# Branch gates by seven products from the fourth unit on, and the silu gate of three retention heads applied as they leave their banks

## The chip, the cores and the metric

The kernel runs on one core of a Trainium2 chip. The metric is device time in microseconds. The kernel before takes 2031.95 us (median of 3 runs, 2031.89 to 2031.98). TensorE is called PE here, VectorE DVE, ScalarE ACT, GpSimd POOL and SyncE SP, as in the profile. Line numbers (L2022) are those of the kernel before.

## The reference, cut to what matters

The reference is one encoder block (attention of two kinds between two feed-forward parts) followed by two hybrid layers and a last norm. 512 tokens, width 1024, float32 throughout. The change touches only the hybrid layers, and of these the end:

```python
a = diff_attention(...) * jax.nn.silu(az)
c = short_conv(cx, cb, cc, conv_w) * jax.nn.silu(cz)
r = retention(rq, rk, rv) * jax.nn.silu(rz)      # retention ends in rms_norm(out) over each head of 128

g = jax.nn.sigmoid(gates).reshape(b, s, 3, 1024) # gates = h @ w_in[:, 5632:], 3072 columns
merged = g[:, :, 0] * (a @ w_branch[0])
for i in range(1, 3):
    merged = merged + g[:, :, i] * (branches[i] @ w_branch[i])
return x + merged @ w_out
```

## The kernel before, in words

**Precision.** Every operand of a large product is kept as a high and a low part (names `_hi`, `_lo`), and a product is three matmuls: high by high, low by high, high by low (L2218 to L2220, and L2351 to L2353 in the seven-product form). A weight slab of 128 x 1024 is loaded by SP into `w_raw` (a ring of six slots), rounded by ACT to `w_hi` (L865), and POOL makes `w_lo = w_raw - w_hi` (L709). `w_lo` lies on the bytes of `w_raw`. SP loads a slab when PE has used the slab that held its slot before (`w_used`).

**The hybrid layer.** It is run twice. Projections and attention come first. Then 16 retention steps run between the convolution's projections: PE adds the outputs of four retention heads in banks 0 to 3, one head of 128 features by 512 tokens in each. Each finished head is squared (`out_squares`, ACT: `r_sq`, a copy of the head to `r_out`, then `sq_hi`), POOL makes `sq_lo`, PE averages the squares into the head's own bank (`mean_square`, L2728 and L2729), ACT takes the square root there (`out_root`), and DVE inverts it, multiplies `r_out` by it and by the silu gate `rz` (`normed_out`, L2022 to L2024). ACT has to load a table each time it changes between square root and sigmoid.

**The merge.** Twelve units follow in each layer. Unit nn handles branch nn mod 3 for a pair of 128-feature blocks: gate columns (two slabs), sigmoid (ACT, into `gate_sb`), branch product (one slab), then DVE multiplies and, for branches 1 and 2, adds (`merged`). A unit is done in one of two ways:

- classic, for nn < M0: two `feature_tile` calls of 8 x 3 matmuls with 512 columns each, 48 in all;
- by seven products, for nn from M0 on: the weight pair and the activations are cut into quarters, sums of quarters of the weights (`gate_w_sums` on DVE, `t_raw1` on POOL) and of the activations (`first_x_sums`, `last_x_sum`, `x_sum_low`, once per layer, DVE) are formed, and seven products of 4 x 3 matmuls with 256 columns replace the eight of the plain form: 84 matmuls. DVE then adds up the partial results before the sigmoids.

`M0` is 4 before. PE in such a unit waits for the low part of the first gate slab (`ready`), for the sums' low parts (`wsl_done`, `xsl_done`), and before the branch product for a low part that belongs to the next unit (`gate_sum_low`, L2140). POOL's `w_lo` for a seven-product unit comes after DVE's `gate_w_sums`, since the sums read `w_raw` (L836).

**Order.** Each engine's list is written out by hand, and engines meet at semaphores only. DVE's list in the first units is: `normed_out(0)`, `normed_out(1)`, then for each nn its extra work and `merged(nn)`; heads 2 and 3 are normed at nn = 1, `retained_low` (`br_lo`, L2016) comes at nn = 2, `first_x_sums` at nn = M0 - 2, and `last_x_sum`, three `x_sum_low`, `gate_w_sums(M0)` and `gate_sum_low(M0, 2)` at nn = M0 - 1. The lines that tie the extra work to M0 are:

```python
if nn == M0 - 2:
    first_x_sums(2 + l, 3 + l, ms_part, ms_raw)
if nn == M0 - 1:
    last_x_sum(2 + l, ms_part, ms_raw)
    ...
    gate_w_sums(M0)
```

Of the kernel before, what the change touches and what calls it, by code (L numbers as in the profile page):

```python
# [15 lines left out]
P = 128  # L16
# [14 lines left out]
M0 = 4  # L31
# [102 lines left out]
def build(nc, x, ffn1_pre_g, ffn1_post_g, ffn1_w_gate, ffn1_w_up, ffn1_w_down, mix_pre_g, mix_post_g,  # L134
# [4 lines left out]
    with ExitStack() as ctx:  # L139
# [215 lines left out]
        swap_in, swap_ready, count_in = sem("swap_in"), sem("swap_ready"), sem("count_in")  # L355
        decay_in = sem("decay_in")
# [45 lines left out]
        mean_ready, rqh_done, rql_done, rst_done, rrt_done = (sem("mean_ready"), sem("rqh_done"), sem("rql_done"),  # L402
# [446 lines left out]
        def _(act):  # L849
# [248 lines left out]
            act.activation(swap_r[:, :], swap_sb[:, :], ACT.Copy).then_inc(swap_ready, 1)  # L1098
# [79 lines left out]
            for l in range(LAYERS):  # L1178
# [98 lines left out]
                def out_squares(h):  # L1277

                    act.wait_ge(r_o_done, 16 * l + 8 * (h // 2) + 7 + h % 2)
                    if h > 0:  # L1280
                        act.wait_ge(rst_done, 4 * l + h)
                    link(act.activation(r_sq[:, :], bank[h][:, :], ACT.Square))
                    act.activation(r_out[:, h, :], bank[h][:, :], ACT.Copy)
                    act.activation(sq_hi[:, :], r_sq[:, :], ACT.Copy).then_inc(rqh_done, 1)
# [14 lines left out]
                for i in range(16):  # L1299
# [30 lines left out]
                    if i in (12, 13, 15):  # L1330
                        out_squares({12: 0, 13: 1, 15: 2}[i])
                out_root(0)
                out_root(1)
                gate(0, 0)
# [93 lines left out]
        def _(dve):  # L1428
# [463 lines left out]
            for l in range(LAYERS):  # L1892
# [196 lines left out]
                normed_out(0)  # L2089
                normed_out(1)  # L2090
# [117 lines left out]
        def _(pe):  # L2208
# [401 lines left out]
            for l in range(LAYERS):  # L2610
# [290 lines left out]
```

## Time and profile before

| what | value |
|---|---|
| median of 3 runs | 2031.95 us (2031.89 to 2031.98) |
| profiled execution, its own time | 2031.64 us |
| its span, first to last instruction | 2029.8 us |
| PE busy | 2013.9 us, 99% of the span |
| DVE busy | 1231.4 us, 61% |
| ACT busy | 953.3 us, 47% |
| POOL busy | 1016.4 us, 50% |
| granted PE clock | 1.000 of full speed |

The profiled execution spends 1.84 us outside its span. A busy share says how much of the span an engine had an instruction in flight. It is an average over stages that differ. A row of a timeline gives the start, the duration (ends of neighbours overlap, so the difference of two starts is the time that an instruction takes in a chain) and, in brackets, idle time before it and what ended it.

### The profile page before, as it was taken

To read this page: it belongs to the slowest core of one execution; us is meant where nothing else is said; L and a number is where in the kernel's file an instruction comes from. 1 tells how busy PE (TensorE), PEld (TensorE's weight loads), DVE (VectorE), ACT (ScalarE), POOL (GpSimd) and SP (SyncE) were. 2 spreads that over 40 slices of the span, in tenths; PEclk is the share of its full clock that TensorE was granted. 3 is DMA by queue.
4 is the path that set the end of the run, shared out by engine and by line. 5 is a ranking of instruction groups with operands and counts; after the bars stand their busy time and mean duration, and the time that the engine had idled before them with its cause. 6 is when DMAs were issued, how large, how long until landed. Compare 5 with 4: busy or idle time off the path is not lost.

```text
span 2029.8 us, 30533 instructions
## 1 busy us (share of the span) xinstructions
PE 2013.9 (99%) x11856; PEld 1752.5 (86%) x11856; DVE 1231.4 (61%) x2036; ACT 953.3 (47%) x1781; POOL 1016.4 (50%) x576
## 2 busy tenths in 40 slices
PE   9999999999999999999999999999999999999998
PEld 8999988877789999988888888899888888888997
DVE  7777730877848777812357573965333676568553
ACT  5454623467755554523444544443443445354442
POOL 4666644346753666744434443465534443264542
PEclk9999999999999999999999999999999999999999
DMA  6333322311133333323322222333332222223332
GB/s 190 107 107 106 104 95 93 123 42 32 32 104 113 107 105 105 104 94 102 121 84 73 73 83 73 94 104 98 111 130 84 83 74 73 83 84 94 105 114 73
DMA packets 244287, 191.65 MB, mean 94 GB/s; under 512 B 6448, under 2 KB 208816, under 8 KB 243760
## 3 DMA queue, kind: packets, MB, share of 16 engines
q1 hardware_dynamic: 244144, 189.70, 30.8%
q8 instruction: 95, 1.56, 0.3%
q14 instruction: 48, 0.39, 0.1%
HBM read 187.58 MB, written 2.10 MB: 93 GB/s over the span
## 4 chain that ended last, share of the span: by engine, by line
PE 94%; DVE 3%; ACT 1%; issue 1%; SPq 0%; DMA 0%; POOL 0%; DVEq 0%; ACTq 0%
PE bank L2218 20%; PE bank L2220 20%; PE bank L2219 20%; PE bank L2353 9%; PE bank L2352 9%; PE bank L2351 9%; PE bank L2212 3%; PE bank L2510 1%; PE bank L2678 1%; PE bank L2530 1%; PE bank L2537 1%; DVE xn L1446 0%; DVE x_tok L1451 0%; PE bank L2707 0%; PE bank L2709 0%
## 5 line engine op out<-in xcount | busy, mean ns | idle before, releaser
L709 POOL TENSOR_TENSOR w_lo<-w_raw,w_hi 128x1024 fp32r<-128x1024 f32 x216 | 533.3, 2480 | 473.8 <-ACT w_hi L865 471.8
L865 ACT ACTIVATE w_hi<-w_raw 128x1024 fp32r<-128x1024 f32 x271 | 283.1, 1053 | 197.1 <-DMA w_raw<-in_ffn_w_down 125.1
L2218 PE MATMUL bank<-xt_hi,w_hi 128*128 128x512 f32 (+1 forms) x640 | 243.3, 380 | 0.5
L2219 PE MATMUL bank<-xt_lo,w_hi 128*128 128x512 f32 (+1 forms) x640 | 239.3, 374 | 0.0
L2220 PE MATMUL bank<-xt_hi,w_lo 128*128 128x512 f32 (+1 forms) x640 | 239.3, 374 | 0.0
L2218 PE MATMUL bank<-w_hi,xt_hi 128*128 128x512 f32 (+1 forms) x456 | 178.2, 391 | 0.0
L2220 PE MATMUL bank<-w_hi,xt_lo 128*128 128x512 f32 (+1 forms) x456 | 174.5, 383 | 0.0
L2219 PE MATMUL bank<-w_lo,xt_hi 128*128 128x512 f32 (+1 forms) x456 | 174.3, 382 | 0.0
L2218 PEld LDWEIGHTS bank<-xt_hi,w_hi 128*128 128x128 f32 x640 | 120.5, 188 | 29.3 <-issue 6.7
L2220 PEld LDWEIGHTS bank<-xt_hi,w_lo 128*128 128x128 f32 x640 | 120.5, 188 | 22.0
L2219 PEld LDWEIGHTS bank<-xt_lo,w_hi 128*128 128x128 f32 x640 | 120.6, 188 | 19.6
L2218 PE MATMUL bank<-w_hi,h_hi 128*128 128x512 f32 x352 | 137.1, 390 | 0.0
L2219 PE MATMUL bank<-w_lo,h_hi 128*128 128x512 f32 x352 | 137.0, 389 | 0.0
L2220 PE MATMUL bank<-w_hi,h_lo 128*128 128x512 f32 x352 | 136.9, 389 | 0.0
L2351 PE MATMUL bank<-xs_hi,ws_hi 128*128 128x256 f32 x456 | 129.0, 283 | 0.0
L2352 PE MATMUL bank<-xs_lo,ws_hi 128*128 128x256 f32 x456 | 129.0, 283 | 0.0
L2353 PE MATMUL bank<-xs_hi,ws_lo 128*128 128x256 f32 x456 | 129.0, 283 | 0.0
L2353 PE MATMUL bank<-xt_hi,w_lo 128*128 128x256 f32 x432 | 122.3, 283 | 0.0
L2352 PE MATMUL bank<-xt_lo,w_hi 128*128 128x256 f32 x432 | 122.2, 283 | 0.0
L2351 PE MATMUL bank<-xt_hi,w_hi 128*128 128x256 f32 x432 | 122.2, 283 | 0.0
L1440 DVE RECIPROCAL stat<-stat 128x1 f32<-128x1 f32 x12 | 2.0, 163 | 185.7 <-ACT stat L889 185.7
L778 POOL TENSOR_TENSOR w_lo<-w_raw,w_hi 128x1024 fp32r<-128x1024 f32 x38 | 91.8, 2415 | 30.9 <-ACT w_hi L865 19.1
(398 smaller groups left out, 5579.4 us busy)
## 6 DMA issues: line engine op xcount, KB each, us to landing
w_raw<-in_w_in SPq DMA_DIRECT2D x132, 512.0 KB, 3.8
w_raw<-in_ffn_w_down SPq DMA_DIRECT2D x44, 512.0 KB, 3.4
w_raw<-in_ffn_w_gate SPq DMA_DIRECT2D x43, 512.0 KB, 3.8
w_raw<-in_ffn_w_up SPq DMA_DIRECT2D x43, 512.0 KB, 3.8
w_raw<-in_w_out SPq DMA_DIRECT2D x24, 512.0 KB, 3.4
w_raw<-in_w_branch SPq DMA_DIRECT2D x24, 512.0 KB, 3.5
w_raw<-in_w_qkv SPq DMA_DIRECT2D x16, 512.0 KB, 3.8
x_tok<-in_x SPq DMA_DIRECT2D x4, 512.0 KB, 6.9
```

What stands on the lines that cost most here:

```text
L709: pool.tensor_tensor(lo_slots[i], raw_slots[i], f32(hi_slots[i]), ALU.subtract).then_inc(lo_ready, 1)
L778: pool.tensor_tensor(lo_slots[i], raw_slots[i], f32(hi_slots[i]), ALU.subtract).then_inc(lo_ready, 1)
L865: act.activation(hi_slots[i], raw_slots[i], ACT.Copy).then_inc(hi_ready, 1)
L2212: ins = pe.matmul(dst[:, cols(k)], blk, ident[:, :], is_transpose=True)
L2218: pe.matmul(out_ap, ah, bh, start=first, stop=False)
L2219: pe.matmul(out_ap, ah, bl, start=False, stop=False)
L2220: return pe.matmul(out_ap, al, bh, start=False, stop=last)
L2351: pe.matmul(dst, wh, xh, start=k == 0 and not onto, stop=False, skip_group_check=onto)
L2352: pe.matmul(dst, wh, xl, start=False, stop=False, skip_group_check=onto)
L2353: ins = pe.matmul(dst, wl, xh, start=False, stop=k == 3, skip_group_check=onto)
L2510: ins = pe.matmul(score_bank(k, e)[:, :], a[rows, cols(c)], b[rows, :], start=part == 0, stop=part == 2)
L2530: ins = pe.matmul(bank[7][:, :].rearrange("p (e q) -> p e q", e=2), va_hilo[:, j, pair // 2, :], p[:, hf, :, j, :], start=j + part == 0, s ...
```

## The change

1. `M0` is 3 instead of 4: unit 3 of each layer is done by seven products. All that is tied to M0 comes one unit earlier: `first_x_sums` joins heads 2 and 3 at nn = 1, and the rest of the preparation joins `retained_low` at nn = 2.
2. For heads 0 to 2 ACT no longer copies the head to `r_out`. DVE writes `r_out = bank * rz` instead (`gated_out`, new semaphore `rg_done`), for heads 0 and 1 at retention steps 13 and 14, for head 2 between `normed_out(0)` and `normed_out(1)`. `mean_square` of these heads, which overwrites the bank, now also waits for `rg_done`. `normed_out` of these heads has one multiplication instead of two.
3. ACT's square roots of heads 0 and 1 stand ahead of `out_squares(2)`.
4. Two one-time semaphores, `swap_ready` and `mean_ready`, become one, `matrix_ready`.

```diff
-M0 = 4
+M0 = 3
...
                     link(act.activation(r_sq[:, :], bank[h][:, :], ACT.Square))
-                    act.activation(r_out[:, h, :], bank[h][:, :], ACT.Copy)
+                    if h == 3:
+                        act.activation(r_out[:, h, :], bank[h][:, :], ACT.Copy)
...
-                    if i in (12, 13, 15):
-                        out_squares({12: 0, 13: 1, 15: 2}[i])
+                    if i in (12, 13):
+                        out_squares(i - 12)
                 out_root(0)
                 out_root(1)
+                out_squares(2)
                 gate(0, 0)
...
                     link(dve.reciprocal(bank[h][:, :], bank[h][:, :]))
+                    if h < 3:
+                        dve.wait_ge(rg_done, 3 * l + h + 1)
+                        dve.tensor_tensor(r_out[:, h, :], bank[h][:, :], r_out[:, h, :], ALU.mult).then_inc(br_ready, 1)
+                        return
                     link(dve.tensor_tensor(r_out[:, h, :], bank[h][:, :], r_out[:, h, :], ALU.mult))
                     dve.tensor_tensor(r_out[:, h, :], r_out[:, h, :], rz[:, h, :], ALU.mult).then_inc(br_ready, 1)
-                    dve.wait_ge(br_ready, 8 * l + 4 + h + 1)
+
+                def gated_out(h):
+
+                    dve.wait_ge(z_done, 8 * l + 4 + h + 1)
+                    dve.wait_ge(rqh_done, 4 * l + h + 1)
+                    dve.tensor_tensor(r_out[:, h, :], bank[h][:, :], rz[:, h, :], ALU.mult).then_inc(rg_done, 1)
...
                         branch_low(i // 2 - 4)
+                    if i in (13, 14):
+                        gated_out(i - 13)
                     dve.wait_ge(r_s_done, 8 * l + i // 2 + 1)
...
                 normed_out(0)
+                gated_out(2)
                 normed_out(1)
...
                     pe.wait_ge(rql_done, 4 * l + h + 1)
+                    if h < 3:
+                        pe.wait_ge(rg_done, 3 * l + h + 1)
```

DVE at retention step 14, before (`ba_lo` is the low part of a turned block of branch a, `ret_a` the scores of this step):

```order
L2011 TENSOR_TENSOR ba_lo<-bank,ba_hi 128x4x128 [waits bth_done]
L2048 TENSOR_TENSOR ret_a<-bank,decay_sb 128x128 [waits r_h_done,r_l_done,r_s_done]
L2065 TENSOR_TENSOR y_sb<-bank,y_sb 128x512 [waits w_used]
L2068 TENSOR_TENSOR y_sb<-y_sb,cz_sb 128x512 [waits cz_done,yb_done]
L2074 TENSOR_TENSOR pt_lo<-ret_a,pt_hi 128x128 [waits r_h_done]
```

and DVE at the same place in the changed kernel (lines are its own):

```order
L2013 TENSOR_TENSOR ba_lo<-bank,ba_hi 128x4x128 [waits bth_done]
L2036 TENSOR_TENSOR r_out<-bank,rz 128x512 [waits rqh_done,z_done]
L2061 TENSOR_TENSOR ret_a<-bank,decay_sb 128x128 [waits r_h_done,r_l_done,r_s_done]
L2078 TENSOR_TENSOR y_sb<-bank,y_sb 128x512 [waits w_used]
L2081 TENSOR_TENSOR y_sb<-y_sb,cz_sb 128x512 [waits cz_done,yb_done]
L2087 TENSOR_TENSOR pt_lo<-ret_a,pt_hi 128x128 [waits r_h_done]
```

`gated_out(1)` stands between `ba_lo`, which PE waits for, and `ret_a`. PE's `mean_square(1)` waits for it too.

DVE from the norm of head 2 on, before: the rows end at the first operation of `merged(1)` (`ms_part` and `ms_raw` are the activation sums, `m_raw` the merged output):

```order
L2022 RECIPROCAL bank<-bank 128x512 [waits rrt_done]
L2023 TENSOR_TENSOR r_out<-bank,r_out 128x512 [waits dve_step]
L2024 TENSOR_TENSOR r_out<-r_out,rz 128x512 [waits dve_step]
L2022 RECIPROCAL bank<-bank 128x512 [waits rrt_done,br_ready]
L2023 TENSOR_TENSOR r_out<-bank,r_out 128x512 [waits dve_step]
L2024 TENSOR_TENSOR r_out<-r_out,rz 128x512 [waits dve_step]
L2107 TENSOR_TENSOR bank<-bank,gate_sb 128x512 [waits gs_done,w_used,br_ready]
```

and DVE there in the changed kernel:

```order
L2024 RECIPROCAL bank<-bank 128x512 [waits rrt_done]
L2027 TENSOR_TENSOR r_out<-bank,r_out 128x512 [waits rg_done,dve_step]
L2024 RECIPROCAL bank<-bank 128x512 [waits rrt_done]
L2029 TENSOR_TENSOR r_out<-bank,r_out 128x512 [waits dve_step]
L2030 TENSOR_TENSOR r_out<-r_out,rz 128x512 [waits dve_step]
L1549 TENSOR_TENSOR ms_part_86<-xt_hi,xt_lo 128x1024 [waits rst_done,xtl_done,r_o_done,ch_done]
L1549 TENSOR_TENSOR ms_part_88<-xt_hi,xt_lo 128x1024
L1564 TENSOR_TENSOR ms_raw_92<-ms_part_86,ms_part_88 128x1024 [waits dve_step]
L1549 TENSOR_TENSOR ms_part_85<-xt_hi,xt_lo 128x1024
L1567 TENSOR_TENSOR ms_raw_89<-ms_raw_92,ms_part_85 128x1024 [waits xs_made,dve_step]
L1568 TENSOR_TENSOR ms_raw_90<-ms_part_85,ms_part_86 128x1024
L2121 TENSOR_TENSOR bank<-bank,gate_sb 128x512 [waits gs_done,w_used]
```

The six operations of `first_x_sums` now stand between the last head and `merged(1)` (L2121 and L2124 there); before, they stood behind `merged(1)` and `retained_low`.

## Rows read from the trace of the kernel before

**Rows 1.** The page: PE's busy time, and the chain that ended last, by engine.
```profile
PE 2013.9 (99%) x11856; PEld 1752.5 (86%) x11856; DVE 1231.4 (61%) x2036; ACT 953.3 (47%) x1781; POOL 1016.4 (50%) x576
...
PE 94%; DVE 3%; ACT 1%; issue 1%; SPq 0%; DMA 0%; POOL 0%; DVEq 0%; ACTq 0%
```

**Rows 2.** Windows, units 1 to 5: length, PE, PEld, DVE, ACT, POOL, clock.
```profile
1275.94:1292.31 16.37, 16.37 (x74) 13.52 (x73) 15.06 (x10) 8.51 (x12) 9.90 (x5) 1.00 0.33 98
1292.31:1308.63 16.32, 16.32 (x74) 13.52 (x73) 15.93 (x14) 3.65 (x5) 9.20 (x4) 1.00 0.32 96
1308.63:1324.95 16.32, 16.32 (x74) 13.52 (x73) 12.70 (x14) 9.62 (x13) 5.51 (x4) 1.00 0.34 98
1324.95:1341.03 16.08, 15.78 (x109) 14.66 (x108) 10.77 (x17) 6.27 (x12) 11.41 (x7) 1.00 0.33 99
1341.03:1356.57 15.54, 15.54 (x109) 14.58 (x108) 9.04 (x16) 6.38 (x12) 9.52 (x7) 1.00 0.33 102
```

**Rows 3.** Waits of PE: total us, times, longest.
```profile
PE bank L2728 <- DVE ba_lo L2011: 0.8, 2, 0.4
PE bank L2218 <- DVE xt_lo L2140: 0.8, 2, 0.5
```

**Rows 4.** Timeline of PE: start, duration, operation, idle before and its releaser.
```profile
1257.39 0.50 PE L2728 MATMUL bank<-sq_hi,mean_r 128*128 128x512 f32 x1 [0.38 <-DVE ba_lo L2011]
```

**Rows 5.** Timeline of DVE, retention step 14.
```profile
1256.64 0.69 DVE L2011 TENSOR_TENSOR ba_lo<-bank,ba_hi 128x512 fp32r<-128x512 f32 x1 [8.03 <-ACT ba_hi L1270]
1257.25 0.28 DVE L2048 TENSOR_TENSOR ret_a<-bank,decay_sb 128x128 f32<-128x128 f32 x1
```

**Rows 6.** Timeline of ACT: squares of head 2, roots of heads 0, 1.
```profile
1263.89 0.60 ACT L1282 ACTIVATE r_sq<-bank 128x512 f32<-128x512 f32 x1 [2.58 <-PE bank L2220]
...
1266.96 1.07 ACT L1288 ACTIVATE bank<-bank 128x512 f32<-128x512 f32 x2
```

**Rows 7.** Timeline of DVE, from head 1 to unit 4.
```profile
1272.49 3.37 DVE L2022 RECIPROCAL bank<-bank 128x512 f32<-128x512 f32 x1
1275.89 0.69 DVE L2023 TENSOR_TENSOR r_out<-bank,r_out 128x512 f32<-128x512 f32 x1
1276.61 2.26 DVE L2024 TENSOR_TENSOR r_out<-r_out,rz 128x512 f32<-128x512 f32 x1
1278.91 1.29 DVE L2105 TENSOR_TENSOR m_raw<-bank,gate_sb 128x512 f32<-128x512 f32 x2
...
1292.56 0.70 DVE L2107 TENSOR_TENSOR bank<-bank,gate_sb 128x512 f32<-128x512 f32 x1 [1.32 <-PE bank L2220]
...
1295.24 4.69 DVE L2016 TENSOR_TENSOR br_lo<-r_out,br_hi 128x512 fp32r<-128x512 f32 x4
1299.85 4.55 DVE L1547 TENSOR_TENSOR ms_part<-xt_hi,xt_lo 128x1024 f32<-128x1024 f32 x2
1304.43 1.22 DVE L1562 TENSOR_TENSOR ms_raw<-ms_part,ms_part 128x1024 f32<-128x1024 f32 x1
...
1307.97 2.31 DVE L1566 TENSOR_TENSOR ms_raw<-ms_part,ms_part 128x1024 f32<-128x1024 f32 x1
...
1319.18 0.70 DVE L2133 TENSOR_TENSOR bank<-bank,w_raw 128x512 f32<-128x512 f32 x1
...
1326.95 0.68 DVE L2140 TENSOR_TENSOR t_lo<-bank,t_hi 128x512 fp32r<-128x512 f32 x1
```

**Rows 8.** Timeline of POOL, same stretch.
```profile
1273.56 12.28 POOL L709 TENSOR_TENSOR w_lo<-w_raw,w_hi 128x1024 fp32r<-128x1024 f32 x5
1292.94 5.23 POOL L709 TENSOR_TENSOR w_lo<-w_raw,w_hi 128x1024 fp32r<-128x1024 f32 x2 [7.09 <-ACT w_hi L865]
1299.57 2.61 POOL L709 TENSOR_TENSOR w_lo<-w_raw,w_hi 128x1024 fp32r<-128x1024 f32 x1 [1.40 <-ACT w_hi L865]
1307.27 1.94 POOL L831 TENSOR_TENSOR t_raw<-w_raw 128x512 f32<-128x512 f32 x1 [5.09 <-DMA w_raw<-in_w_in]
1320.02 3.25 POOL L836 TENSOR_TENSOR w_lo<-w_raw,w_hi 128x1024 fp32r<-128x1024 f32 x1 [10.81 <-DVE bank L2133]
```

More of the change, by code:

```diff
@@ L354, in build @@
         tabs1_in, tabs2_in = sem("tabs1_in"), sem("tabs2_in")
-        swap_in, swap_ready, count_in = sem("swap_in"), sem("swap_ready"), sem("count_in")
-        decay_in = sem("decay_in")
+        swap_in, matrix_ready, count_in = sem("swap_in"), sem("matrix_ready"), sem("count_in")
+        decay_in, rg_done = sem("decay_in"), sem("rg_done")
         ident_ready = sem("ident_ready")
@@ L401, in build @@
         fl_done = sem("fl_done")
-        mean_ready, rqh_done, rql_done, rst_done, rrt_done = (sem("mean_ready"), sem("rqh_done"), sem("rql_done"),
+        rqh_done, rql_done, rst_done, rrt_done = (sem("rqh_done"), sem("rql_done"),
                                                               sem("rst_done"), sem("rrt_done"))
@@ L1097, in _ @@
             act.wait_ge(swap_in, 48)
-            act.activation(swap_r[:, :], swap_sb[:, :], ACT.Copy).then_inc(swap_ready, 1)
+            act.activation(swap_r[:, :], swap_sb[:, :], ACT.Copy).then_inc(matrix_ready, 1)
             highs(S_UNIT)
@@ L2034, in _ @@
                 link(dve.memset(u_sb[:, 0:2], 0.0))
-                dve.memset(f32(mean_r[:, :]), 1.0 / P).then_inc(mean_ready, 1)
+                dve.memset(f32(mean_r[:, :]), 1.0 / P).then_inc(matrix_ready, 1)
                 dve.wait_ge(decay_in, 16 * (l + 1))
@@ L2557, in unit_swap @@
                 if j == 0:
-                    pe.wait_ge(swap_ready, 1)
+                    pe.wait_ge(matrix_ready, 1)
                 pe.wait_ge(uc_done, j + 1)
@@ L2725, in mean_square @@
                     if h == 0:
-                        pe.wait_ge(mean_ready, l + 1)
+                        pe.wait_ge(matrix_ready, l + 2)
                     pe.wait_ge(rql_done, 4 * l + h + 1)
+                    if h < 3:
+                        pe.wait_ge(rg_done, 3 * l + h + 1)
                     pe.matmul(bank[h][:, :], mean_r[:, :], sq_hi[:, :], start=True, stop=False)
```

## The prediction, made before the change was timed

> **What bounds the kernel now.** I read the page first: PE is busy 99% of the span, and 94% of the chain that ended last is PE's [rows 1]. So a change is worth what it takes from PE's own work, less what it adds to PE's waits. Then I cut layer 0's merge into windows of one unit, because that is where M0 acts [rows 2]. Units 1 to 3 are classic and last 16.32 us (unit 1: 16.37). Unit 5, by seven products, lasts 15.54. Unit 4, the first by seven products, lasts 16.08: 0.54 over unit 5. The same rows show DVE busy 15.06 and 15.93 of 16.3 us in units 1 and 2, and 12.70 in unit 3, the unit that goes. So DVE, idle over much of the kernel, is full just where the change takes a unit of cover away. The waits of PE [rows 3] give two places where DVE is late already, each twice (once a layer): `mean_square` behind `ba_lo`, and the branch product of the first seven-product unit behind L2140. After that I followed DVE and POOL row by row. All rows are of layer 0; layer 1 has the same waits at the same places, so the sum is made once and doubled.
>
> **PE's own work.** Unit 3 goes from 48 matmuls of 512 columns to 84 of 256. The windows have both kinds with the branch product in them: 16.32 - 15.54 = 0.78 us less a layer [rows 2]. The Trainium skill ("TensorE: Matmul & The Clock Gate", Back-to-back issue gap) gives the isolated spacing as N / 2.4 plus 2.5 ns: 109.2 ns for 256 columns, 215.8 for 512, so 48 x 215.8 - 84 x 109.2 = 1.19 us, an estimate by that page. By it the sum below would be 0.8 us lower over two layers. The windows measure the pair in this kernel, so 0.78 stands.
>
> **`gated_out(1)` before `mean_square(1)`.** PE starts L2728 at 1257.39, just behind `ba_lo`, which starts at 1256.64 and takes 0.69 [rows 4, 5]. Now `gated_out(1)` stands next on DVE. It starts where `ret_a` started, 0.61 after `ba_lo`, and I give it 0.69, as L2023, which also reads one bank and one SBUF tile [rows 7]. PE is released 0.61 us later. PE had no slack there, so this is a plain cost. Bounds: 0 if `ba_lo` were not the last releaser, 0.75 if it takes its whole duration. I take 0.61.
>
> **`gated_out(0)` and `gated_out(2)`: nothing.** Head 0's waits for `sq_hi`, which ACT now reaches sooner by one copy, and DVE is idle 8.03 us between steps 13 and 14 [rows 5]; that gap covers it. If it did not, the cost would be another 0.7. Head 2's follows `normed_out(0)`. ACT was idle for 2.58 us before the squares of head 2, that is from 1261.3 [rows 6]; three operations of some 0.6 and a table load, which fills the 1.3 us that are left up to 1266.96, preceded the roots. Now the load and the roots use the idle time: 1261.3 + 0.6 (`gated_out(1)` has moved DVE, and ACT behind it) + 1.3 = 1263.2, the first root 0.6 later. The reciprocal (3.40) and its multiplication (0.7) follow, so `gated_out(2)` ends near 1268.7, and PE's third mean square begins at about 1270 (unit 0's product of 24 matmuls and this stand before 1275.94). The squares of head 2 stay near 1264.4, since PE releases them, 0.6 later than before. The table loads are as many as before. That leaves 1.4 us of slack before it costs anything.
>
> **DVE's list up to the first seven-product unit.** Before, `merged(0)` began at 1278.91 because the two heads ahead of it were late [rows 7]; PE was through with that product about 1275.5. Now two multiplications and the 1.6 us that one of them lost (2.26 against 0.69 [rows 7]) are gone, so DVE waits for PE: 1275.5 + 0.61 + 0.25 (the lag seen at unit 1, 1292.56 against 1292.31 [rows 2, 7]) = 1276.3. From there, with differences of starts [rows 7]: `merged(0)` 1.2, to 1277.5. Heads 2 and 3: 3.40 + 0.72 and 3.40 + 0.72, to 1285.7, then head 3's last multiplication beside the end of POOL's five `w_lo` (1273.56 + 12.28 = 1285.84 [rows 8]), to 1286.5. Then comes, without a gap, everything from `first_x_sums` to `gate_w_sums`. Before, this ran from 1299.85 to 1319.18 + 0.70 = 1319.88: 20.03 us, one `merged` of four operations in it, as now. `retained_low` is added to it.
>
> Two sizes in it need a choice. The first two sums took 4.55 where their like takes 1.2 (the row at 1304.43), an excess of 2.1; `br_lo` took 4.69 for four, where 0.61 each makes 2.45, an excess of 2.2 [rows 5, 7]. Both lie beside POOL's `w_lo` [rows 8] (the instructions at 1292.94 and 1299.57). In the changed kernel POOL's run of `w_lo` has ended by 1285.84, and its next is held until `gate_w_sums` is done. The bounds are no excess and all of it, 4.3; I take none. L1566's excess of 1.1 beside `t_raw` stays, because `t_raw` falls into the same stretch. So 20.03 - 2.1 + 2.45 = 20.4, and `gate_w_sums` ends at 1306.9. The Trainium skill ("SBUF — State Buffer", Who interferes with whom) says that a DVE instruction with two SBUF inputs and a GpSimd one that reads SBUF exclude each other for a whole instruction. The trace agrees in that L2024 took 2.26 beside POOL's `w_lo`, while operations with a bank input there kept 0.69. By that rule the excess goes, by a reading as a lasting property of these operations it stays; the second is the rival below.
>
> **What PE then waits for in unit 3.** Without waits PE starts it at 1308.63 + 0.61 = 1309.24 [rows 2].
> - The low part of the first gate slab: POOL had it 3.39 us after `gate_w_sums` (1319.88 to 1320.02 + 3.25 [rows 7, 8]), and PE started unit 4 at 1324.95, 1.7 us later still. Now it is there at 1306.9 + 3.4 = 1310.3: PE waits 1.1.
> - The third product needs the last sums' low parts, behind `merged` on DVE. `merged(3)` had two operations (1.2); `merged(2)` has four (1292.56 to 1295.24, 2.68). From 1309.24 + 0.25: 2.68 + 1.2 = 1313.4. PE is there two products (2.9) after its start, 1313.2: 0.2. Had the first wait been nothing, this one would be 1.3. The two together cost 1.3 either way, so the term does not hang on the 20.4 being exact: it may be 1 us shorter without changing anything.
> - The branch product, late by 0.54 before. The low parts ended 2.68 after the unit's start (1326.95 + 0.68 [rows 7]); now 2.85 after, with the 0.2 taken off. I take 0.6, bounds 0.3 and 0.9.
>
> **The sum, a layer.** -0.78 + 0.61 + (1.3 + 0.6 - 0.54) = +1.2 us. Two layers: +2.4. On the profiled execution 2031.64 + 2.4 = 2034.0; its median stands 0.3 above it, so 2034.3. A measurement of this kernel is taken to tell a change from none at 0.2%, 4.1 us; +2.4 is inside that. The semaphore that replaces two others costs nothing: its writers are a cast from before the attention and a memset ahead of the 16 retention steps, the reader is at the fourteenth.
>
> **Rivals.**
> 1. *DVE's excess stays* (slower). The place is `first_x_sums` and `retained_low`; the price is 2.1 for one of the two or 4.3 for both, a layer, and it decides once DVE's list is over 1 us longer than my 20.4, since it is then all of PE's wait at the first gate slab. Time: 2034.3 + 2 x 2.1 = 2038.5, or 2042.9 for both. For it: no row shows these operations with POOL quiet in the hybrid layers; POOL's list shifts too, and one instruction misplaced is 1 us. Against it: every such excess in the rows has a POOL instruction beside it. 0.14.
> 2. *The gain comes and the waits do not*. If the sums are ready in unit 3 as they are in unit 5, a layer saves 0.78 + 0.54, less the 0.61: 0.7, so 2030.5; without the 0.61 too, 2029.3. For it: three multiplications and one contended wait are off DVE. Against it: `merged(2)` cannot begin before PE ends the branch product, and its four operations and two low parts are longer than two products. 0.12.
> 3. *The `rg_done` wait is free*, the rest as forecast: 2034.3 - 1.2 = 2033.1. For it: only if DVE lets PE go on as early as before; against it rows 4 and 5. 0.08.
>
> The forecast itself has 0.66, with 2032.8 to 2035.8 as its own range (0.3 to 0.9 for the branch wait, 0 to 0.75 for `rg_done`, 0.3 for each of the others). Faster by over 0.2% is under 2027.9, which even rival 2 does not reach: 0.02 for what I have not seen. Slower is over 2036.0: rival 1 and a little of the forecast's tail, 0.15. Within: 0.83. The range for 8 in 10 is 2031.8 to 2037.5: it leaves out most of rival 2 and the far half of rival 1.
>
> **What would show it.** In the profile of the changed kernel: the window of unit 3 between 16.5 and 17.8 us and unit 4 at 15.5; a wait of L2728 behind the new DVE line of `gated_out`, twice; a wait of the first matmul of unit 3 for POOL's `w_lo`; `br_lo` x4 in 2.5 us and the sums in 1.2 each; `gate_w_sums` of unit 3 ending 1.5 to 3 us before PE wants to start. Wrong: unit 3 at 15.6 us (rival 2), or `br_lo` and the sums as long as before with POOL idle and unit 3 near 19 (rival 1).

## The result, and the profile after

The changed kernel takes 2036.91 us (median of 11 runs, 2036.76 to 2037.21) against 2031.95 of the kernel before: 5.0 us longer, a ratio of 1.0025 with the interval 1.0017 to 1.0032. (One of the 11 runs of the kernel before was disturbed and took 8432.89 us; the ten others lie between 2031.74 and 2032.08.) The forecast was 2034.3. The time is inside the range of 2031.8 to 2037.5 and outside the forecast's own range of 2032.8 to 2035.8. The interval leaves no doubt that the kernel is slower; whether by more than the 0.2% that the prediction set as its mark is open, since 1.0020 lies inside the interval. The profiled execution took 2036.89 us with a span of 2034.9.

The page's rows of PE's busy time and of the chain that ended last, as [rows 1]:

```profile
PE 2013.6 (99%) x11928; PEld 1754.9 (86%) x11928; DVE 1232.4 (61%) x2060; ACT 955.8 (47%) x1789; POOL 1018.9 (50%) x580
...
PE 91%; DVE 5%; ACT 2%; issue 1%; SPq 0%; DMA 0%; POOL 0%; DVEq 0%; POOLq 0%; ACTq 0%
```

PE is busy for 0.3 us less than before, in a span that is 5.1 us longer. (The ends of matmuls are modelled and reach into short waits: the window of unit 3 below has 16.11 us of PE where unit 5 needs 15.54. The 0.3 is therefore less than what the seven products save.) The chain says where that went: PE's share fell from 94% to 91%, DVE's rose from 3% to 5%. The same windows as [rows 2], units 1 to 5 of layer 0 (length, PE, PEld, DVE, ACT, POOL, clock):

```profile
1276.64:1293.00 16.36, 16.36 (x73) 13.51 (x72) 16.19 (x12) 8.00 (x11) 10.54 (x5) 1.00 0.32 97
1293.00:1310.50 17.50, 16.48 (x73) 13.33 (x71) 16.48 (x21) 9.62 (x13) 3.28 (x2) 1.00 0.30 91
1310.50:1328.10 17.60, 16.11 (x108) 14.80 (x109) 12.60 (x18) 6.27 (x12) 14.05 (x8) 1.00 0.31 90
1328.10:1343.64 15.54, 15.54 (x109) 14.58 (x108) 7.65 (x14) 6.38 (x12) 9.47 (x7) 1.00 0.33 102
1343.64:1359.18 15.54, 15.54 (x109) 14.58 (x108) 9.05 (x16) 6.37 (x12) 8.60 (x6) 1.00 0.35 102
```

Read against [rows 2], the table gives the account of a layer without a remainder. Unit 1 starts 0.70 later than before. Unit 2 is 1.18 longer. Unit 3 is 1.28 longer, although its work by seven products is 0.78 shorter, so it holds 2.06 of waits. Unit 4 is 0.54 shorter. 0.70 - 0.01 (unit 1) + 1.18 + 1.28 - 0.54 = 2.61 us, and unit 5 starts at 1343.64 instead of 1341.03. Twice that is 5.2; the profiled executions differ by 2036.89 - 2031.64 = 5.25. The clock stood at 1.00 throughout, the 2.4 GHz level.

The waits of PE, as [rows 3] (us in total, times, longest). In this kernel L2744 is the `mean_square` matmul (L2728 before), L2232 the first of `three` (L2218), L2365 the first of `product` (L2351), L2154 is `gate_sum_low` (L2140):

```profile
PE bank L2232 <- DVE xt_lo L2154: 3.0, 2, 1.5
...
PE bank L2744 <- DVE r_out L2036: 2.1, 2, 1.1
PE bank L2365 <- POOL w_lo L836: 2.0, 2, 1.0
```

The three of them in the timeline of PE, in layer 0; the first row answers to [rows 4]:

```profile
1258.12 0.47 PE L2744 MATMUL bank<-sq_hi,mean_r 128*128 128x512 f32 x1 [1.06 <-DVE r_out L2036]
...
1310.50 0.39 PE L2365 MATMUL bank<-xt_hi,w_hi 128*128 128x256 f32 x1 [1.02 <-POOL w_lo L836]
...
1322.54 0.47 PE L2232 MATMUL bank<-ba_hi,w_hi 128*128 128x512 f32 x1 [1.49 <-DVE xt_lo L2154]
```

All three places are those that the prediction named; the wait at the branch product, the third, was 0.8 in all before and is 3.0. What DVE does on the way there, as [rows 5] and [rows 7]:

```profile
1257.30 0.68 DVE L2036 TENSOR_TENSOR r_out<-bank,rz 128x512 f32<-128x512 f32 x1
...
1267.72 0.68 DVE L2036 TENSOR_TENSOR r_out<-bank,rz 128x512 f32<-128x512 f32 x1
...
1276.36 1.29 DVE L2119 TENSOR_TENSOR m_raw<-bank,gate_sb 128x512 f32<-128x512 f32 x2 [3.95 <-PE bank L2234]
...
1286.82 2.35 DVE L1549 TENSOR_TENSOR ms_part<-xt_hi,xt_lo 128x1024 f32<-128x1024 f32 x2
...
1291.59 2.35 DVE L1567 TENSOR_TENSOR ms_raw<-ms_raw,ms_part 128x1024 f32<-128x1024 f32 x1
...
1297.66 2.49 DVE L2018 TENSOR_TENSOR br_lo<-r_out,br_hi 128x512 fp32r<-128x512 f32 x4
...
1306.39 0.70 DVE L2147 TENSOR_TENSOR bank<-bank,w_raw 128x512 f32<-128x512 f32 x1
1306.99 1.22 DVE L1582 TENSOR_TENSOR ms_lo<-ms_raw,ms_hi 128x1024 fp32r<-128x1024 f32 x1
...
1310.26 0.69 DVE L2124 TENSOR_TENSOR m_raw<-bank,m_raw 128x512 f32<-128x512 f32 x1
...
1314.02 2.38 DVE L1582 TENSOR_TENSOR ms_lo<-ms_raw,ms_hi 128x1024 fp32r<-128x1024 f32 x1
1316.33 1.78 DVE L2143 TENSOR_TENSOR bank<-w_raw 128x512 f32<-128x512 f32 x1
1318.14 0.70 DVE L2145 TENSOR_TENSOR bank<-bank,w_raw 128x512 f32<-128x512 f32 x1
...
1321.71 0.68 DVE L2154 TENSOR_TENSOR xt_lo<-bank,xt_hi 128x512 fp32r<-128x512 f32 x1
```

POOL beside it, as [rows 8]:

```profile
1307.22 3.23 POOL L836 TENSOR_TENSOR w_lo<-w_raw,w_hi 128x1024 fp32r<-128x1024 f32 x1 [14.35 <-DVE bank L2147]
...
1312.92 2.40 POOL L709 TENSOR_TENSOR w_lo<-w_raw,w_hi 128x1024 fp32r<-128x1024 f32 x1
1315.28 2.27 POOL L831 TENSOR_TENSOR t_raw<-w_raw 128x512 f32<-128x512 f32 x1
```

and, in the kernel before, the slab of the branch product that POOL's run ends with (its `t_raw` and DVE's `ms_lo` of that time are under e1):

```profile
1325.72 2.42 POOL L709 TENSOR_TENSOR w_lo<-w_raw,w_hi 128x1024 fp32r<-128x1024 f32 x1
```

Up to 1307 everything runs as it was worked out. `merged(0)` waits for PE (3.95 idle before it), the four `br_lo` take 2.49 where they took 4.69, `gate_w_sums` ends at 1307.09, and POOL has the slab's low part at 1310.45. The loss is at the end of both blocks. `ms_lo` (the last of the activations' low parts) starts at 1314.02 and takes 2.38 where [rows 7] have its like at 1.2: it ends 1.1 after POOL's slab does (1315.32). `t_raw` on POOL takes 2.27 instead of 1.29 and ends 1.2 after `ms_lo`. The first sum of unit 4's weights, L2143, takes 1.78 instead of 0.69 and ends 0.6 after `t_raw`. Each waits for the one before it, three times over, and PE's branch product waits for what stands behind L2143.

The Trainium skill ("SBUF — State Buffer", Who interferes with whom) has this rule, and adds that issue order decides who blocks. The rows agree: `ms_lo` and L2143, each with two SBUF inputs, end 1.1 and 0.6 after the POOL instruction that had begun before them, about the time that either takes by itself. `merged(2)`, whose four operations have one input in a bank, stands beside POOL's run from 1309.52 to 1312.28 and keeps 0.69 to 0.70 in each (L2124 above).

### The profile page after: what moved, and what is told of

The parts are those of the page before. It is cut to its first block, busy times and chain, and to the rows that moved or that the text cites. A ratio compares the mean times of both kernels' runs of the same rounds, so it can differ in the third digit from the quotient of the medians.

```text
span 2034.9 us, 30757 instructions
## 1 busy us (share of the span) xinstructions
PE 2013.6 (99%) x11928; PEld 1754.9 (86%) x11928; DVE 1232.4 (61%) x2060; ACT 955.8 (47%) x1789; POOL 1018.9 (50%) x580
## 4 chain that ended last, share of the span: by engine, by line
PE 91%; DVE 5%; ACT 2%; issue 1%; SPq 0%; DMA 0%; POOL 0%; DVEq 0%; POOLq 0%; ACTq 0%
PE bank L2232 19%; PE bank L2233 18%; PE bank L2234 18%; PE bank L2365 9%; PE bank L2367 9%; PE bank L2366 9%; PE bank L2226 3%; PE bank L2524 1%; PE bank L2692 1%; PE bank L2544 1%; DVE bank L2024 1%; PE bank L2551 1%; DVE xn L1448 0%; DVE x_tok L1453 0%; PE bank L2721 0%
## 5 line engine op out<-in xcount | busy, mean ns | idle before, releaser
L709 POOL TENSOR_TENSOR w_lo<-w_raw,w_hi 128x1024 fp32r<-128x1024 f32 x212 | 522.8, 2476 | 459.9 <-ACT w_hi L865 459.5
L2232 PE MATMUL bank<-xt_hi,w_hi 128*128 128x512 f32 (+1 forms) x608 | 230.9, 380 | 0.5
L2233 PE MATMUL bank<-xt_lo,w_hi 128*128 128x512 f32 (+1 forms) x608 | 226.9, 373 | 0.0
L2234 PE MATMUL bank<-xt_hi,w_lo 128*128 128x512 f32 (+1 forms) x608 | 226.8, 373 | 0.0
L2232 PE MATMUL bank<-w_hi,xt_hi 128*128 128x512 f32 (+1 forms) x456 | 178.2, 391 | 0.0
L2232 PEld LDWEIGHTS bank<-xt_hi,w_hi 128*128 128x128 f32 x608 | 114.5, 188 | 28.2 <-issue 6.7
L2232 PE MATMUL bank<-w_hi,h_hi 128*128 128x512 f32 x352 | 137.1, 390 | 0.0
L2234 PEld LDWEIGHTS bank<-xt_hi,w_lo 128*128 128x128 f32 x608 | 114.5, 188 | 20.7
L2233 PEld LDWEIGHTS bank<-xt_lo,w_hi 128*128 128x128 f32 x608 | 114.6, 189 | 18.4
L2365 PE MATMUL bank<-xs_hi,ws_hi 128*128 128x256 f32 x456 | 129.0, 283 | 0.0
L2365 PE MATMUL bank<-xt_hi,w_hi 128*128 128x256 f32 x448 | 126.9, 283 | 2.0 <-POOL w_lo L836 2.0
L2367 PE MATMUL bank<-xt_hi,w_lo 128*128 128x256 f32 x448 | 126.8, 283 | 0.0
L2366 PE MATMUL bank<-xt_lo,w_hi 128*128 128x256 f32 x448 | 126.8, 283 | 0.0
L778 POOL TENSOR_TENSOR w_lo<-w_raw,w_hi 128x1024 fp32r<-128x1024 f32 x38 | 91.8, 2415 | 30.9 <-ACT w_hi L865 19.1
```

Of the source, the lines that this page charges most:

```text
L709: pool.tensor_tensor(lo_slots[i], raw_slots[i], f32(hi_slots[i]), ALU.subtract).then_inc(lo_ready, 1)
L778: pool.tensor_tensor(lo_slots[i], raw_slots[i], f32(hi_slots[i]), ALU.subtract).then_inc(lo_ready, 1)
L2232: pe.matmul(out_ap, ah, bh, start=first, stop=False)
L2233: pe.matmul(out_ap, ah, bl, start=False, stop=False)
L2234: return pe.matmul(out_ap, al, bh, start=False, stop=last)
L2365: pe.matmul(dst, wh, xh, start=k == 0 and not onto, stop=False, skip_group_check=onto)
```

## Experiments

"Before" below is the kernel before, run on the same chip beside each group. Its median was 2031.76 beside e1 to e4, 2031.68 beside e5 to e8, 2031.80 beside e9 to e12 and 2031.95 beside the changed kernel, so a difference between kernels of two groups is uncertain by up to 0.3 us. Line numbers in a kernel's own rows are shifted by a few from those of the changed kernel.

### e1: the head part alone

```
-M0 = 3
+M0 = 4
```

> The head part of the change alone: M0 back at 4, everything else as in the changed kernel. Theory (the wait for rg_done is a plain cost, and the head part gives nothing back while M0 is 4): 0.68 us more a layer at mean_square(1), nothing else, so 2031.95 + 1.4 = 2033.3, and the branch product of the first seven-product unit still 0.54 late. Rival (the shorter VectorE list is worth something by itself): 2032 or less.

Measured: 2031.82 us (2031.61 to 2031.96) against 2031.76, a ratio of 1.0000 (0.9991 to 1.0009). PE waits the same 1.1 at `mean_square(1)`. What I had missed is that the 0.54 at the branch product of unit 4 goes. POOL's and DVE's rows there:

```profile
1327.65 1.29 POOL L831 TENSOR_TENSOR t_raw<-w_raw 128x512 f32<-128x512 f32 x1
```

```profile
1329.26 1.22 DVE L1582 TENSOR_TENSOR ms_lo<-ms_raw,ms_hi 128x1024 fp32r<-128x1024 f32 x1
```

`t_raw` ends at 1328.94, ahead of `ms_lo`, which keeps its 1.22. The same two in the kernel before, POOL and DVE:

```profile
1328.08 1.30 POOL L831 TENSOR_TENSOR t_raw<-w_raw 128x512 f32<-128x512 f32 x1
```

```profile
1328.36 2.11 DVE L1580 TENSOR_TENSOR ms_lo<-ms_raw,ms_hi 128x1024 fp32r<-128x1024 f32 x1
```

So that 0.54 was a meeting of DVE and POOL too, not a list that is too long. Two shifts made them pass each other. With three multiplications less, `gate_w_sums` ends 0.46 sooner and `t_raw` begins 0.43 sooner. And unit 4, with `ms_lo` behind it, begins 0.90 later (1325.85 against 1324.95), 0.68 of which is the new wait at `mean_square(1)`. The later unit is the larger part: neither shift alone would have parted the two. A layer: +0.68 - 0.54, about nothing.

### e2: M0 alone, in the kernel before

```
-M0 = 4
+M0 = 3
```

> M0 = 3 alone, heads as before. Theory (VectorE's list up to gate_w_sums decides): the heads end at 1291.2 as before, the 20.4 us list follows, gate_w_sums ends near 1311.7, POOL's low part of the first gate slab near 1315.1, so TensorE waits 6.5 us a layer for it in place of 1.2, and the branch wait is 0.9: about +6.1 a layer, 2044. Rival (the seven-product unit costs what it costs, the heads do not matter for it): the changed kernel less its rg_done wait, 2035.5.

Measured: 2046.32 us (2046.02 to 2046.92, 5 runs), 1.0072 (1.0058 to 1.0086): 14.6 us over before. Its waits of PE, and four windows in a row from PE's wait ahead of unit 3 (first row) through its first two products and the third (columns as above):

```profile
PE bank L2351 <- POOL w_lo L836: 9.4, 2, 4.9
PE bank L2218 <- DVE br_lo L2016: 2.6, 2, 1.3
```

```profile
1311.00:1315.29 4.29, 0.00 (x0) 0.00 (x0) 4.22 (x7) 2.51 (x4) 3.26 (x2) 0.82 0.41 122
1315.29:1318.02 2.73, 2.73 (x12) 2.73 (x13) 2.16 (x4) 0.00 (x0) 2.73 (x3) 0.50 0.00 0
1318.02:1320.58 2.56, 2.56 (x13) 2.56 (x13) 0.00 (x0) 1.85 (x3) 2.56 (x2) 0.50 0.02 6
1320.58:1322.04 1.46, 1.46 (x14) 1.46 (x13) 1.24 (x2) 0.00 (x0) 0.72 (x1) 0.99 0.00 0
```

Without the head part, `gate_w_sums` ends at 1311.90 and PE stands still for 4.9 us; then it runs its first two products in 5.29 us instead of 2.88, at a granted clock of 0.50. The expected 6.5 us of delay ahead of unit 3 came (1.3 of it at the branch product of unit 2, for `br_lo`); the expected wait at the branch product of unit 3 didn't, in layer 0. The lower clock cost 2.4 us there and was not foreseen, and 2044 was 2.3 too low. So the head part is worth nothing at M0 = 4 (e1) and 2046.32 - 2036.91 = 9.4 us at M0 = 3. The two parts can't be priced one by one.

### e3: `gated_out(1)` at the end of DVE's step 13

```
-                    if i in (13, 14):
-                        gated_out(i - 13)
+                    if i == 13:
+                        gated_out(0)
...
+                    if i == 13:
+                        gated_out(1)
                     if i == 0:
```

> The changed kernel with gated_out(1) moved to the end of retention step 13, into VectorE's idle time, instead of behind the low part of branch a at step 14. Theory: the wait at mean_square(1) goes back to the 0.4 us it had, 0.68 less a layer, 2036.9 - 1.4 = 2035.5. Rival (the later work is paced by VectorE, not TensorE, so a sooner TensorE only waits longer for the first gate slab): the 0.68 is given back there, 2036.9.

Measured: 2035.54 us (2035.31 to 2035.76), 1.0019 (1.0010 to 1.0027): 1.4 us less than the changed kernel. The wait is that of [rows 3] again:

```profile
PE bank L2746 <- DVE ba_lo L2013: 0.8, 2, 0.4
```

The other two waits are as long as in the changed kernel. That is the `rg_done` term by itself: 0.7 a layer.

### e4: POOL's next slab held behind the weight sums

```
+                    if nn == M0:
+                        pool.wait_ge(ws_made, 3 * q + 6)
                     lows(g + 2, g + 3)
```

> The changed kernel with POOL held, in the first seven-product unit only, before the low part of the branch slab until VectorE has made the next unit's weight sums. Theory (in unit 3 VectorE's ms_lo, 2.38 us for 1.22, and its first weight sum, 1.78 for 0.69, wait for POOL's instructions, 2.2 us together, and that is the 1.65 us by which the branch product is late): both are short, the branch wait is gone, 1.65 less a layer, 2033.6. Rival (VectorE's list behind merged(2) is too long as such): the branch product stays over 1 us late, 2036 to 2037.

Measured: 2033.55 us (2033.35 to 2033.73), 1.0009 (1.0000 to 1.0018): 3.4 us less than the changed kernel. The same stretch on DVE and on POOL:

```profile
1314.17 1.22 DVE L1584 TENSOR_TENSOR ms_lo<-ms_raw,ms_hi 128x1024 fp32r<-128x1024 f32 x1
1315.31 0.69 DVE L2145 TENSOR_TENSOR bank<-w_raw 128x512 f32<-128x512 f32 x1
```

```profile
1317.54 2.41 POOL L709 TENSOR_TENSOR w_lo<-w_raw,w_hi 128x1024 fp32r<-128x1024 f32 x1 [4.44 <-DVE bank L2149]
```

With POOL out of the way `ms_lo` takes 1.22 and the first sum 0.69. The branch product's wait for `xt_lo` is gone from the list of waits, and unit 4 starts at 1326.53 instead of 1328.10. The slab that POOL makes 4.6 us later is not missed by anyone. This shows that the whole of the branch wait was the turns of DVE and POOL, and not the length of DVE's list.

### e5: the squares of head 2 back ahead of the roots

```
-                    if i in (12, 13):
-                        out_squares(i - 12)
+                    if i in (12, 13, 15):
+                        out_squares({12: 0, 13: 1, 15: 2}[i])
                 out_root(0)
                 out_root(1)
-                out_squares(2)
```

> The changed kernel with the square roots of heads 0 and 1 behind the squares of head 2 again. Theory (gated_out(2) stands behind normed_out(0), and mean_square(2) waits for it): the first root ends near 1268.3, the reciprocal and two multiplications near 1273, TensorE waits for them from 1270.2 on, 2.8 us a layer, 2042.5. Rival (the 1.4 us of slack and the idle time of VectorE cover it): 2036.9, at most 2038.

Measured: 2041.95 us (2041.78 to 2045.07, 5 runs), 1.0055 (1.0043 to 1.0068): 5.0 us over the changed kernel. Three of the five lie at 2041.78 to 2041.95, the others at 2043.32 and 2045.07. The profiled run is the longest. The first wait of PE, and two windows: PE's wait ahead of the third mean square, and a stretch of the products behind it:

```profile
PE bank L2743 <- DVE r_out L2035: 6.8, 4, 2.3
```

```profile
1269.92:1272.70 2.78, 0.45 (x4) 0.32 (x3) 2.75 (x4) 0.80 (x2) 0.00 (x0) 1.00 0.46 135
...
1275.00:1277.00 2.00, 2.00 (x6) 1.52 (x6) 1.52 (x2) 1.97 (x3) 1.67 (x2) 0.50 0.00 0
```

With the roots behind the squares, `gated_out(2)` ends at 1272.56 and PE's third mean square waits 2.3 us for it. The new order of ACT is thus what makes `gated_out(2)` free. The mean square starts 2.5 later than in the changed kernel (1272.71 against 1270.18), and twice 2.5 is the whole 5.0 of the median. In the profiled run the clock falls behind the wait as well, and the product of 24 matmuls after it takes 7.08 instead of 5.48; layer 1 is the same, and these 3.2 us are what this run has over the three short ones.

### e6: the last activation sum behind `merged(2)`, the weights' low parts ahead of it

```
                         gate_w_sums(M0)
-                        x_sum_low(2 + l, 1, 3, ms_hi, ms_lo, ms_raw)
-                        gate_sum_low(M0, 2)
+                        for m in (2, 3, 4):
+                            gate_sum_low(M0, m)
                     merged(nn)
-                gate_sum_low(M0, 3)
-                gate_sum_low(M0, 4)
+                x_sum_low(2 + l, 1, 3, ms_hi, ms_lo, ms_raw)
```

> The changed kernel with VectorE's low parts of all three weight sums of unit 3 ahead of merged(2) and the low part of activation sum 1 behind it. Theory (POOL's slab low part, 3.23 us, had waited for that activation sum; without it the first gate slab is there 0.85 sooner and the third product waits for nothing; but 1.2 us and a wait for POOL are added behind merged(2), where the branch product is late already): first wait 0.3, branch wait 2.7, sum unchanged, 2036 to 2037. Rival (the first wait is what counts): 0.9 to 1.2 less a layer, 2034.8.

Measured: 2038.90 us (2037.27 to 2040.58, 6 runs), 1.0033 (1.0021 to 1.0045). That is 1.9 above the upper end of what I expected. POOL's first slab is quicker as meant, for no `ms_lo` stands beside it, and unit 3 starts 0.83 sooner. But now two `ms_lo` meet POOL's run:

```profile
1312.21 3.36 DVE L1582 TENSOR_TENSOR ms_lo<-ms_raw,ms_hi 128x1024 fp32r<-128x1024 f32 x1
...
1315.83 1.96 DVE L1582 TENSOR_TENSOR ms_lo<-ms_raw,ms_hi 128x1024 fp32r<-128x1024 f32 x1
```

The branch product waits 2.3 us, and runs at half clock behind the wait (the profiled run is the longest of the six). The six times are 2037.27, 2037.43, 2038.80, 2039.01, 2039.09 and 2040.58; the two shortest are only 0.4 to 0.5 over the changed kernel. The wait was expected (2.7), the fall of the clock was not. The wait's end and the product's start in windows:

```profile
1320.40:1322.80 2.40, 0.14 (x2) 0.00 (x1) 2.04 (x4) 1.54 (x5) 2.40 (x2) 0.98 0.34 95
1322.83:1325.00 2.17, 2.17 (x5) 1.78 (x6) 1.79 (x4) 1.13 (x4) 2.04 (x2) 0.50 0.44 132
```

### e7 and e8: the three edits together, with M0 = 3 and M0 = 4

```
+ e3's edit (gated_out(1) in step 13)
+ e4's edit (POOL holds lows(g + 2, g + 3) for nn == M0)
+ e6's edit (low parts of the weight sums ahead of merged(M0 - 1))
  M0 = 3 in e7, M0 = 4 in e8
```

> The changed kernel with all three edits: gated_out(1) sooner, POOL held, low parts of the sums ahead of merged(2). Theory: waits of a layer are 0.4 at mean_square(1) as before the change, 0.3 at the first slab, 0 at the third product, 0.4 at the branch product, so -0.78 + 0.3 + 0.4 - 0.54 = -0.6 a layer against the kernel before, 2030.7. Rival (the three waits are one and the last of them stays): 2033 to 2035.

> The same three edits with M0 = 4. Theory: only the 0.54 us wait of a layer is left to gain, 2030.9, the same as with M0 = 3 within 0.5 us. Rival (the seven-product unit 3 is worth its full 0.78 a layer once nothing waits): 1.5 us slower than the kernel with M0 = 3.

Measured: e7 2030.32 us (2030.13 to 2030.50), 0.9993 (0.9985 to 1.0002); e8 2030.37 us (2030.23 to 2030.57), 0.9994 (0.9985 to 1.0002), against 2031.68 of the kernel before. The stretch in e7, DVE, then POOL, then unit 3 as a window:

```profile
1311.46 1.21 DVE L1584 TENSOR_TENSOR ms_lo<-ms_raw,ms_hi 128x1024 fp32r<-128x1024 f32 x1
...
1312.93 1.21 DVE L1584 TENSOR_TENSOR ms_lo<-ms_raw,ms_hi 128x1024 fp32r<-128x1024 f32 x1
```

```profile
1306.45 2.41 POOL L836 TENSOR_TENSOR w_lo<-w_raw,w_hi 128x1024 fp32r<-128x1024 f32 x1 [13.22 <-DVE bank L2151]
```

```profile
1308.92:1324.75 15.83, 15.83 (x108) 14.74 (x109) 11.00 (x18) 6.38 (x12) 10.82 (x7) 1.00 0.33 100
```

Unit 3 lasts 15.83, POOL's first slab 2.41 instead of 3.23, and both `ms_lo` 1.2. The edit of e6, worth +2.0 by itself (+0.4 in its shortest runs), is worth -1.85 on top of the other two (e9 below): the same move meets POOL in one kernel and misses it in the other. e8 has no wait of the merge left in its list, and unit 4 is at 15.54. Yet the two are equal: M0 = 3 has 0.78 less work a layer and 0.3 + 0.3 of waits that M0 = 4 has not, which leaves under 0.2. In layer 0, unit 5 starts at 1340.29 in e7 and at 1340.39 in e8.

### e9: e3 and e4 only

```
+ e3's edit
+ e4's edit
```

> The changed kernel with two of the edits, gated_out(1) sooner and POOL held, VectorE's order before and behind merged(2) as changed. Theory (the edits' gains add up): 2036.9 - 1.4 - 3.3 = 2032.2, level with the kernel before. Rival (the third edit gives nothing once POOL is held): the 2030.3 of the kernel with all three.

Measured: 2032.17 us (2031.96 to 2032.46), 1.0002 (0.9993 to 1.0011). The gains of e3 (1.37) and e4 (3.36) add up to 4.7; the two together give 4.7. They are independent, and together they are back at the kernel before.

### e10 and e11: head 3 gated from its bank too

```
-                    if h < 3:
-                        dve.wait_ge(rg_done, 3 * l + h + 1)
+                    dve.wait_ge(rg_done, 4 * l + h + 1)
...
-                    dve.tensor_tensor(r_out[:, h, :], r_out[:, h, :], rz[:, h, :], ALU.mult).then_inc(br_ready, 1)
...
                 normed_out(1)
+                gated_out(3)
  on top of e7 (e10) and of e8 (e11)
```

> All three edits with M0 = 3, and head 3 treated as the other heads: VectorE multiplies its gate in from the bank in its idle time ahead of merged(0), ScalarE's copy and one multiplication are gone. Theory (VectorE's list up to gate_w_sums is 1.2 us shorter, TensorE had waited 0.33 for the first slab and lost 0.1 restarting): 0.4 less a layer, 2029.5. Rival (the first slab was not late by VectorE's list): 2030.3.

> The same with M0 = 4. Theory (no wait is left there that the shorter list could take away): 2030.4 as with the three edits, and so about 0.9 above M0 = 3, the first measured worth of the seven-product unit. Rival: the same time as with M0 = 3, 2029.5 to 2030.4.

Measured: e10 2030.31 us (2030.01 to 2030.49), 0.9993 (0.9984 to 1.0002), 0.01 from e7 and 0.8 above what I expected; e11 2030.86 us (2030.71 to 2031.02), 0.9995 (0.9987 to 1.0004). In e10 the wait for the first slab is gone and unit 3 starts at 1308.60, 0.32 sooner than in e7, but a wait that e7 had lost comes back at the branch product. The first operation of `merged(2)` and that wait:

```profile
1308.80 0.70 DVE L2120 TENSOR_TENSOR bank<-bank,gate_sb 128x512 f32<-128x512 f32 x1 [0.52 <-PE bank L2232]
```

```profile
PE bank L2230 <- DVE xt_lo L2153: 0.7, 2, 0.4
```

DVE is now early and waits for PE at `merged(2)`, which begins at 1308.80 (1308.79 in e7, without a wait). Everything behind it runs at the same times as in e7, and unit 5 starts at 1340.29 in both. From the start of unit 3 to the end of that `xt_lo` (1318.36 + 0.68 = 1319.04) DVE and ACT need 10.44 us, and PE's seven products of 1.44 need 10.08: this is what is left of the prediction's argument against rival 2. e11 is 0.55 above e10, which ran beside it, where I expected 0.9; every run of e11 is longer than the longest of e10. Between the starts of units 1 and 5 of layer 0 e10 is 0.16 shorter (64.38 against 64.54), the same as between e7 and e8 (64.39 and 64.55). So some 0.3 of the 0.55 is what the seven-product unit 3 is worth in both layers once nothing but the branch product waits; the rest lies outside these units. Why e11 is 0.5 above e8 wasn't looked into with a run of its own. Its waits for `xn`, outside the merge, are 2.7 us in all against 2.1, which is of the right size, but not shown as the cause.

### e12: only `t_raw` held, not the slab

```
+                    if nn == M0 + 1:
+                        pool.wait_ge(ws_made, 3 * q + 3)
                     wait_raw(pool, g)
```

> The changed kernel with only POOL's t_raw of the second seven-product unit moved behind VectorE's weight sums of that unit. Theory (POOL and VectorE take turns, each waiting for the other's whole instruction: ms_lo waits for w_lo, t_raw for ms_lo, the first weight sum for t_raw): the first weight sum falls from 1.78 to 0.69, ms_lo stays near 2.4, the branch wait falls by 1.1 to 0.55, 2034.7. Rival (the first weight sum is slow for its own reasons, such as the bank): 2036.9.

Measured: 2034.82 us (2034.55 to 2034.92), 1.0015 (1.0006 to 1.0023): 2.1 us less than the changed kernel, out of e4's 3.4.

```profile
1314.12 2.38 DVE L1584 TENSOR_TENSOR ms_lo<-ms_raw,ms_hi 128x1024 fp32r<-128x1024 f32 x1
1316.43 0.69 DVE L2145 TENSOR_TENSOR bank<-w_raw 128x512 f32<-128x512 f32 x1
```

The chain of turns is cut in the middle. `ms_lo` still waits for POOL's slab (2.38), but the weight sum behind it keeps 0.69, and 0.55 of the branch wait is left, counted from where the seventh product ends. The link between `t_raw` and the sum is shown by this run alone, the one between the slab and `ms_lo` by e4, where both are gone. That `t_raw` itself waits for `ms_lo` (2.27 against 1.29) is read from the rows only.

## Why the prediction came out as it did

The account of a layer, predicted beside measured (us):

| step | predicted | measured |
|---|---|---|
| PE's own work, unit 3 by seven products | -0.78 | -0.78 |
| `gated_out(1)` ahead of `mean_square(1)` | +0.61 | +0.68 |
| unit 3's first slab, POOL's low part | +1.1 | +1.18 |
| the third product (0.21), and the first product, 0.10 slower behind its wait | +0.2 | +0.31 |
| the branch product (with the slower start behind the wait) | +0.6 | +1.75 |
| the branch wait of before, gone | -0.54 | -0.54 |
| sum | +1.2 | +2.6 |

- **PE's own work** was right: unit 3 of 17.60 less its waits (0.31 + 1.75) is 15.54, the length of unit 5; its products behind the third take 1.44 each, as unit 5's do. The prediction's estimate from the isolated spacing of the Trainium skill ("TensorE: Matmul & The Clock Gate", Back-to-back issue gap), 1.19, is not borne out: 256 columns take 120 ns here (12 in 1.44 us) and 512 columns 227 (24 in 5.44).
- **`gated_out(1)`** was right in place and size; e3 takes just this wait away and gains 1.4 in two layers. Rival 3 (that it is free) fell.
- **`gated_out(0)` and `gated_out(2)` cost nothing**, as said: the roots start at 1263.03 (predicted 1263.2), `gated_out(2)` ends at 1268.40 (1268.7). The reason given, ACT's idle time ahead of the squares of head 2, is shown by e5: without it PE waits 2.3 us.
- **DVE's list** was right: `gate_w_sums` ends at 1307.09 (1306.9). The excess of `br_lo` and of the first sums went, and that of L1567 stayed (2.35, beside the `t_raw` that POOL runs from 1291.57). So rival 1, that the excess is a property of the operations, fell.
- **Unit 3's start and third product** were right: POOL's low part at 1310.45 (1310.3), 1.49 for the two (1.3). But the 3.4 that the prediction gave POOL for that slab was carried over from the rows of before with a meeting in it: the slab takes 3.23 beside the `ms_lo` at 1306.99, and 2.41 in e7, where that `ms_lo` stands elsewhere. So 0.8 of this wait is of the same kind as the one that was missed, and came out right because the change left that pair together.
- **The branch product is the step that failed.** The prediction reads: "The low parts ended 2.68 after the unit's start [rows 7]; now 2.85 after, with the 0.2 taken off. I take 0.6, bounds 0.3 and 0.9". The place was right, the term was taken from how late DVE's list had been, and it measured 1.75. What ties it is POOL's run. Before, that run began at 1320.02, 4.93 ahead of unit 4 (1324.95), and its slab (L709, from 1325.72 for 2.42) ended 3.2 after the unit's start, just ahead of `ms_lo`, which so met only the `t_raw` behind it, for 0.9. Now the run begins at 1307.22, 3.28 ahead of unit 3, since PE itself waits for its first slab; so POOL's run lies 1.65 later against the unit, and its slab ends 4.8 after the start. `ms_lo`, which starts 3.5 after the unit, meets the slab, and the sum behind it meets `t_raw`. e4 takes both collisions away and with them the whole wait; e12 takes one; e1 shows that the 0.54 of before was of this kind. The trace of the kernel before had the rows for it: the prediction moved POOL's run to 1307, checked only its first slab, and did not lay the four instructions behind it over DVE's list. It named this danger ("POOL's list shifts too, and one instruction misplaced is 1 us") under a rival at another place, and gave it no place in the sum.
- **Rival 2** (the gain comes, the waits don't, 2030.5) did not happen in this kernel, but its time is where e7, e8 and e10 end up, once the waits are edited away. There too most of unit 3's 0.78 is given back; in e10 that is because the work of DVE and ACT from the start of unit 3 to the branch product's `xt_lo` is 0.4 longer than PE's products.

Within 0.2% had a chance of 0.83; the median lies 0.9 us beyond that bound. That it is inside the range for 8 in 10 is luck: the part above 2035.8 stood there for rival 1, which did not happen. The mechanism that filled it had no place in the range. The term's upper bound should have held one stretch of `ms_lo` more, by what it can be held (0.9 + 1.2 = 2.1 a layer). The sum would then have been up to 1.5 a layer higher, 2037.3, and 2036.9 inside the forecast's own range.

The best of the kernels measured are e10 (2030.31), e7 (2030.32) and, with M0 = 4, e8 (2030.37). They are 1.3 to 1.5 us below the kernel before beside them and 6.5 to 6.6 below the changed one. The intervals of their ratios to the kernel before reach 1.0002, so by those they are not told from it, though each of their 33 runs is shorter than every run of the kernel before beside them.

## What to carry to other kernels

When a change moves the start of one engine's run, lay the whole run, to its last instruction, over the other engines' lists, not only the result that is waited for first: here the slab that PE waited for was forecast within 0.15 us, and the instructions behind it cost 1.15 a layer more than forecast. A short wait that is already there should be traced to the collision that makes it before it is extrapolated; its size says little of what it becomes when the offset changes. And edits around such meetings don't always add: two did (e9), and a third was worth +2.0 alone and -1.85 on top of them. Look at the single times too: a median of six that lie 3.3 apart hid two effects in that +2.0.

## What the hardware showed that I had not expected

**The clock behind a wait.** In the changed kernel PE's waits of 1.0 to 1.5 us left the granted clock of all five units at 1.00. Behind the waits of 2.3 us in e5 and e6 and of 4.9 us in e2 the windows above show 0.50, the 1.2 GHz level. Before it fell, PE had done next to nothing for the length of the wait, and before it rose again it had run without a gap. The price beside the wait itself, in layer 0: 2.41 us in e2 (5.29 for two products of 2.88), 1.6 in e5 (7.08 for 5.48) and 1.5 in e6 (7.09 for 5.56).

The traces of e5 and e6 are of the longest run of each, and the other runs say that the clock does not fall every time. Both kernels have one such wait a layer, two in all. The times of e5 lie at 2041.8 to 2042.0 (three), 2043.3 and 2045.1, those of e6 at 2037.3 to 2037.4 (two), 2038.8 to 2039.1 (three) and 2040.6: steps of about 1.6, as if it fell behind none, one or both of the waits. Only one execution of each kernel was traced, so this is a reading of the times and not shown. It would explain why they lie 3.3 us apart, and the runs of kernels without such waits 0.3 to 0.5. By it a wait of 2.3 us costs its own length in one run and some 4 us in another; a forecast that adds waits up linearly can be too low there, and a median of few runs can fall on either.

**Turns in a row.** That DVE and POOL hold each other up stood in the rows of before; that three instructions in a row, on alternating engines, each waited for the one before and so carried a delay from POOL's slab to the weight sum (1315.32, 1316.40, 1317.55, 1318.11, the four ends in the changed kernel) did not.
